# Five of eight heads' retrieval queries and half of an embedding gate moved between the expert rows of block 0; eight gather slots outside the activations

## What is computed

```
q = (h @ w_q).reshape(B, S, 8, 2, 128)
s1, s2 = q[..., 0, :] @ sub_k1, q[..., 1, :] @ sub_k2      # scores against 128 keys each
v1, i1 = top_k(s1, 16); v2, i2 = top_k(s2, 16)
top_s, pos = top_k(v1[..., :, None] + v2[..., None, :], 16)  # 16 experts a head
wts = softmax(top_s)
act = gelu(einsum('thkd,td->thk', u_tab[idx], h))
out = einsum('thk,thkd->td', act * wts, v_tab[idx])
ple = sigmoid(h @ ple_gate) * (p @ ple_proj)
h = layer_norm(alpha * h + out + ple)
```

## Time and profile before

| | us |
|---|---|
| median of 3 runs (2114.31 to 2115.43) | 2114.32 |
| the profiled execution's own time | 2115.31 |
| its span, first to last instruction | 2113.5 |
| PE busy | 1796.5 (85%) |
| DVE busy | 1407.9 (67%) |
| ACT busy | 992.0 (47%) |
| POOL busy | 765.5 (36%) |

### The profile page before, as it was taken

How to read it: one execution, slowest core, us unless ns; L and a number is a source line. 1 busy time by engine, 2 the same in 40 slices (tenths; PEclk the granted TensorE clock), 3 DMA queues, 4 the chain that set the end, 5 groups by cost and what they waited for, 6 DMA issues and landing times.

```text
span 2113.5 us, 29001 instructions
## 1 busy us (share of the span) xinstructions
PE 1796.5 (85%) x6952; PEld 1054.8 (50%) x6952; DVE 1407.9 (67%) x3374; ACT 992.0 (47%) x2295; POOL 765.5 (36%) x614
## 2 busy tenths in 40 slices
PE   8999999978787787787799899998888877878876
PEld 7988778822232222222289887787323322323222
DVE  5864555677777677776558645566777776777764
ACT  5644354454554544444346443444445454444443
POOL 0020000146555556655400300001565655665553
PEclk9999999999999999999999999999999999999999
DMA  7422445789999999999844233456899999999997
GB/s 259 145 101 92 138 140 190 276 354 428 427 427 428 427 427 428 427 428 427 371 137 144 90 110 130 151 188 249 352 427 428 428 427 427 427 427 428 428 427 319
DMA packets 106126, 659.43 MB, mean 312 GB/s; under 512 B 11824, under 2 KB 11968, under 8 KB 39616
## 3 DMA queue, kind: packets, MB, share of 16 engines
q0 software_dynamic: 75232, 545.52, 61.5%
q1 hardware_dynamic: 30816, 112.91, 15.8%
HBM read 657.32 MB, written 1.06 MB: 312 GB/s over the span
## 4 chain that ended last, share of the span: by engine, by line
DMA 22%; PE 21%; issue 9%; DVE 5%; ACT 5%; POOL 2%; DVEq 0%; POOLq 0%; ACTq 0%
DMA arena<-experts_dram,stage 17%; PE acc L593 7%; DMA hidden<-experts_dram,stage 4%; PE psum L544 4%; PE psum L546 3%; PE psum L545 3%; DVE arena L1273 1%; ACT arena L924 1%; POOL arena L510 1%; DVE arena L1244 1%; ACT gw L921 1%; ACT w_hi L858 1%; DMA raw<-weights_dram 1%; POOL stage L507 1%; DVE arena L1117 1%
## 5 line engine op out<-in xcount | busy, mean ns | idle before, releaser
L593 PE MATMUL acc<-arena 128*128 128x512 f32 x1536 | 764.0, 628 | 233.8 <-ACT arena L924 224.8
L510 POOL DMA_INDIRECT arena<-experts_dram,stage x384 | 526.1, 1370 | 342.5 <-PE acc L593 223.0
L1244 DVE CUSTOM_DVE_ANT_0 arena<-arena,h 128x1024 f32<-128x1024 f32 x384 | 471.1, 1227 | 248.0 <-DMA arena<-experts_dram,stage 162.3
L593 PEld LDWEIGHTS acc<-arena 128*128 128x128 f32 x1536 | 273.8, 194 | 715.2 <-issue 714.8
L918 ACT ACTIVATE gel<-dots 128x1 f32<-128x1 f32 x512 | 103.3, 202 | 520.3 <-DVE dots L1244 519.5
L1152 DVE TENSOR_TENSOR raw_r<-raw,w_hi 128x1024 fp32r<-128x1024 f32 x200 | 237.1, 1222 | 148.9 <-ACT w_hi L858 147.9
L858 ACT ACTIVATE w_hi<-raw 128x1024 fp32r<-128x1024 f32 x200 | 203.7, 1055 | 158.6 <-DMA raw<-weights_dram 128.2
L593 PE MATMUL acc<-hidden,arena 128*128 128x512 f32 x512 | 245.0, 612 | 29.8 <-ACT arena L924 27.4
L924 ACT ACTIVATE arena<-cst,gw 128x128 f32<-128x128 f32 x512 | 205.8, 402 | 87.7 <-ACT gw L921 37.0
L510 POOL DMA_INDIRECT hidden<-experts_dram,stage x128 | 163.7, 1279 | 137.3 <-PE acc L593 95.5
L1244 DVE CUSTOM_DVE_ANT_0 hidden<-hidden,h 128x1024 f32<-128x1024 f32 x128 | 157.3, 1229 | 74.5 <-issue 45.8
(11 more groups left out here) (256 smaller groups left out, 2052.3 us busy)
## 6 DMA issues: line engine op xcount, KB each, us to landing
raw<-weights_dram SPq DMA_DIRECT2D x208, 512.0 KB, 3.4
arena<-experts_dram,stage POOLq DMA_INDIRECT x384
lnr<-lnrows_dram POOLq DMA_DIRECT2D x4, 1024.0 KB, 5.3
arena<-cum_dram POOLq DMA_DIRECT2D x2, 1024.0 KB, 9.3
hidden<-experts_dram,stage POOLq DMA_INDIRECT x128
cst<-consts_dram SPq DMA_DIRECT2D x1, 1640.0 KB, 15.3
par<-params_dram POOLq DMA_DIRECT2D x2, 616.0 KB, 11.1
h<-x_dram SPq DMA_DIRECT2D x2, 512.0 KB, 5.4
```

The source lines that it names most:

```text
L510: nc.gpsimd.indirect_dma_start(slots[i % RING][:, :], None, experts[:, :], bass.IndirectOffsetOnAxis(stage[:, i:i + 1], 0)).then_inc(slot_ ...
L593: last = mm(acc[:, c * 512:(c + 1) * 512], diag[:, i % 4, :], slots[i % RING][:, D + c * 512:D + (c + 1) * 512], start=False, stop=ends)
L1244: nc.vector.tensor_tensor_reduce(slots[s][:, 0:D], slots[s][:, 0:D], h[:, b, :], 1.0, 0.0, ALU.mult, ALU.add, dots[:, i:i + 1]).then_inc(d ...
```

## The change

- `steps()`: head by head. Three heads' queries and scores come first, each head in two half steps (`wqh`, `wq`) and two score steps (`sc`, b, head), with `select` 0 and 1 between them; then the first half of the gate, in quarters (`pgw`), and then the 128 rows of block 0 as steps of their own. Beside head r of them stand head r + 3's half steps after rows 3 and 6 and its scores after row 9 (r from 0 to 4), and beside head 5 the gate's other half after rows 3, 6, 9 and 12. Block 1 stays in the loop.
- `group_list()`: the pieces come in that order; keys in four half pieces of 256 KB. High halves stand at rows 0 and 2, low halves at rows 1 and 3 of a head.
- The rows of block 0 are straight code on every engine; POOL reads `idxu` directly, without the copy to `stage`.
- Slots 6 and 7 are no longer in `hidden`, for both blocks: one lies in the arena, one over 2048 columns of the constants, which only the dense stage reads. POOL reloads them (1 MB) after the last row of layer 0, and the users in layer 1 wait for it (`dense_consts`). The queries keep four tiles, used in turn, outside the slots.
- POOL's waits for the last scores and the last gate product go; what is left are the head's indices and `row_used`. DVE waits for a head's scores where it selects.

```diff
-    s += [("wq", 0, 0), ("pp", 1, 1), ("wq", 0, 1), ("wq", 1, 0), ("wq", 1, 1)] + [("sc", b, g) for g in range(2) for b in range(2)]
-    s += [("select", 0), ("texp", 0), ("wq", 2, 0), ("wq", 2, 1), ("wq", 3, 0), ("wq", 3, 1)]
-    s += [("sc", b, g) for g in range(2, 4) for b in range(2)]
-    s += [("pg", 0, 0), ("pg", 0, 1), ("select", 1), ("texp", 1), ("pg", 1, 0), ("pg", 1, 1)]
-    s += [("experts", 0), ("ln2", 0), ("experts", 1), ("ln2", 1)]
+    s += [("wqh", 0, 0), ("wq", 0, 0), ("pp", 1, 1), ("sc", 0, 0), ("sc", 1, 0), ("select", 0)]
+    s += [("wqh", 0, 1), ("wq", 0, 1), ("sc", 0, 1), ("sc", 1, 1), ("texp", 0), ("select", 1)]
+    s += [("wqh", 1, 0), ("wq", 1, 0), ("sc", 0, 2), ("sc", 1, 2), ("texp", 1)]
+    s += [("pgw", 0, j) for j in range(4)] + [("pg", 0, 0), ("pg", 0, 1)]
+    beside = {(hd - 3, 3): [("wqh", hd // 2, hd % 2)] for hd in range(3, EH)}
+    beside |= {(hd - 3, 6): [("wq", hd // 2, hd % 2)] for hd in range(3, EH)}
+    beside |= {(hd - 3, 9): [("sc", 0, hd), ("sc", 1, hd)] for hd in range(3, EH)}
+    beside |= {(5, 3 + 3 * j): [("pgw", 1, j)] for j in range(4)}
+    beside[5, 12] += [("pg", 1, 0), ("pg", 1, 1)]
+    for r in range(EH):
+        for i in range(TOPK):
+            s += [("row", r, i)] + beside.get((r, i), [])
+    s += [("ln2", 0), ("experts", 1), ("ln2", 1)]
...
+    put_splits(at, ("wq", 1, 0), (("wq", 0, 1), ("wq", 0, 1)))
+    put_splits(at, ("pg", 0, 0), (("texp", 0), ("texp", 0), ("texp", 1), ("texp", 1)))
...
-        slots += [hidden[:, 2 * D * i:2 * D * (i + 1)] for i in range(2)]
-        qpT = at(4096, 4096).rearrange("p (k t) -> p k t", k=16)
+        slots += [at(15648, 2 * D), cst[:, C_LEV:C_LEV + 2 * D]]
+        qpT = at(20320, 1024).rearrange("p (k t) -> p k t", k=4)
...
+                    if kind == "row":
+                        _, r, i = step
+                        n = r * TOPK + i
+                        if i == 0:
+                            pool.wait_ge(idx_ready, L * NB * EH + r + 1)
+                        pool.wait_ge(row_used, L * NB * RANKS + n + 1)
+                        nc.gpsimd.indirect_dma_start(
+                            slots[n % RING][:, :], None, experts[:, :],
+                            bass.IndirectOffsetOnAxis(idxu[:, n:n + 1], 0)).then_inc(slot_in[n % RING], 16)
...
+                        pool.wait_ge(acc_filled, NB * (L + 1))
+                        pool.dma_start(cst[:, C_LEV:C_LEV + 2 * D], consts[:, C_LEV:C_LEV + 2 * D]).then_inc(consts_back, 16)
...
+                        act.wait_ge(dot_ready, n0 + n + 1)
+                        AC(gel[:, i:i + 1], dots[:, i:i + 1], ACT.Gelu).then_inc(dot_used, 1)
+                        act.wait_ge(dot_used, n0 + n + 1 + TOPK)
+                        link(AC(gw[:, i:i + 1], gel[:, i:i + 1], ACT.Copy, scale=wts[:, n:n + 1]))
+                        act.wait_ge(row_used, n0 + n + RING - 3)
+                        AC(diag[:, i % 4, :], ident, ACT.Copy, scale=gw[:, i:i + 1]).then_inc(diag_ready, 1)
```

More of the change, by code:

```diff
@@ L173, with dense_splits @@
 COUNTED = [(i, j) for i, j in PIECES if GROUPS[i][2][j] is None]
-def splits():
-    order = [i for i, g in enumerate(GROUPS) if g[1]]
+def dense_splits(lo):
+    order = [i for i, g in enumerate(GROUPS) if g[1] and g[0][0][0] not in ("wq", "pg")]
     at = {}
@@ new lines, in feature_major, with gate_piece @@
+            def feature_major(L, g, ps, p):
+                feature_half(L, g, ps, 2 * p, 0)
+                return feature_half(L, g, ps, 2 * p + 1, 1)
+            def gate_piece(L, c, j, blocks):
+                w = split(L, GROUP_OF["pg", c, 0], j)
+                for ps, b in blocks:
+                    for i in range(2):
+                        k = 2 * j + i
+                        ends[b] = mm3(ps, [hT[:, i2, k, b * P:(b + 1) * P] for i2 in range(2)], [x[:, i * 512:(i + 1) * 512] for x in w], k == 0, k == KT - 1)
+                read(L, GROUP_OF["pg", c, 0], j, ends[1])
@@ L1224, in _ @@
                         continue
+                    if kind == "row":
+                        _, r, i = step
+                        n = r * TOPK + i
+                        if i == 0:
+                            choose = select_head(L, r + AHEAD)
+                        dve.wait_ge(dot_used, L * NB * RANKS + n + 1)
+                        dve.wait_ge(*landed(L, n))
+                        slot = slots[n % RING]
+                        nc.vector.tensor_tensor_reduce(slot[:, 0:D], slot[:, 0:D], h[:, 0, :], 1.0, 0.0, ALU.mult, ALU.add, dots[:, i:i + 1]).then_inc(dot_ready, 1)
+                        if i == 0:
+                            if r + AHEAD < EH:
+                                dve.wait_ge(*drained(L, ("sc", 0, r + AHEAD)))
+                            elif r + AHEAD == EH:
+                                for hd in range(EH):
+                                    dve.wait_ge(*drained(L, ("sc", 1, hd)))
+                        next(choose, None)
+                        if i == TOPK - 1:
+                            for _ in choose:
+                                pass
+                        continue
                     if kind == "experts":
@@ L1227, in _ @@
                         n0 = (L * NB + b) * RANKS
-                        g0 = (L * NB + b) * EH
-                        for q in range(1, 8):
-                            dve.wait_ge(*drained(L, ("sc", q % 2, q // 2)))
                         def head(r, beside, looped):
```

214 lines of the change are left out of this document (132 added, 82 removed).

## The result

| | before | after |
|---|---|---|
| median of the runs, us | 2114.32 (4 runs, 2113.12 to 2115.43) | 2087.85 (4 runs, 2086.63 to 2089.71) |
| profiled execution: own time, span | 2115.31, 2113.5 | 2088.15, 2086.3 |
| PE / DVE / ACT / POOL busy | 1796.5 / 1407.9 / 992.0 / 765.5 | 1783.1 / 1404.2 / 942.9 / 724.9 |
| moved, mean over the span | 659.43 MB, 312 GB/s | 660.72 MB, 317 GB/s |

The ratio is 0.9874, with a 95% interval from 0.9858 to 0.9889: faster by 26.5 us, where I had forecast 30.5. The last pair of experiments adds that the same program gained only 17.6 us in a later measurement.

What follows compares the result with a forecast made beforehand. Gathers filling the DMA engines, started late, were taken as the bound. Two restarts 41.2 us earlier, less 43.9 for pieces and 4 a layer for gaps, gave 30.5 off 2114.32: 2084 us, own range 2075 to 2096, whole range 2064 to 2108.

Steps and rivals of the forecast that it cites:

- restart: Ninth gather of a layer, first needing a slot freed by PE: 41.2 us earlier in each layer (394.4, not 435.6).
- pieces: Weight loads still to be issued after the restart, 20 in layer 0, 13 in layer 1, at 1.33 us: cost 43.9 us.
- plateau: Stretch of some 600 us per layer, from the restart on, with the 16 DMA engines full at 427 to 428 GB/s.
- gaps: DMA time lost to dense work on PE, 3 us just after the restart and 1 in head 5: 4 us a layer.
- slack of 3 us either way: Uncertainty given to the chain up to the restart, chiefly which half VectorE gets to first: some 3 us.
- Only the restart in the sum: The start's gain was counted by the restart's move alone, 41.2 us a layer; earlier first gathers were not priced.
- The hand-offs: At each drain of queries or scores beside the rows, PE waits 2.2 us for ACT's drain and three small operations.
- Costed at nothing: VectorE's low halves, ACT's high halves, the 1 MB constants reload, the fourth key piece and the unrolled code: 0 us.
- Fully covered: Rival, chance 0.2: no gap after the restart and pieces at 428 GB/s, gain 42 us, 2072 us.
- Thin gain: Rival, chance 0.17: pieces at 1.55 us, 10 us of gaps a layer, or a chain 3 us later; 2103 us.
- The row chain: Rival, chance 0.07: drains empty the ring, dense time is exposed and row work becomes the bound; slower, about 2140 us.

Runs made afterwards that it cites:

- The last pair of experiments: The changed kernel unaltered, and one with the gate's second half spread over heads 5 and 6, run together on another chip: 2096.57 and 2095.94 us.
- experiment 2: The changed kernel with the first gather held until the first half of the gate is in its banks: 2105.79 us.
- experiment 8: The changed kernel with the whole gate beside the rows and VectorE's two operations on a drained gate bank behind the next row's dot: 2070.50 us.
- experiment 1: The kernel before with only its two last slots moved, the constants reloaded, and no wait for the gate ahead of the seventh gather: 2117.54 us.

## Why the prediction was right, and where it was off

The mechanism was right: an earlier restart, paid for with pieces in the plateau. That the sum was only 3.3 us off, by the spans, is in part luck: the restarts gave 3.1 us more than I had and the pieces cost 3.3 less, and the gaps cost 9.7 more. Layer 0's last gather came 11.7 us earlier, where I had 11, by the same cancelling; layer 1's came a further 15.5, where I had 20.

- **The restart, 41.2 us.** Right: 44.0 and 41.5. The steps stood as told: first gather 360.2 (361.3), second selection's halves 374.9 (376.0), row 0's dot 383.9 (386.5). The last quarter of the gate ended 0.8 us sooner than I had it, and the first sigmoid and its two operations ran beside that quarter and the second sigmoid, where I had them one after the other; from dot to restart it took 7.7 us (7.9). But "slack of 3 us either way" was too small: on the last chip the restart comes 4.4 us later in layer 0 (1.6 of it ahead of the first gather) and 3.6 in layer 1, and 17.6 us of gain are left in place of 26.5. At 2096.57 us the same program lies just above the forecast's own range of 2075 to 2096, though within the whole range, which ends at 2108.
- **Only the restart in the sum.** Right for this change, wrong as a measure: experiment 2 moves the restart by 4.2 and the layer by 9.0 us. It held since the first eight gathers had landed when the ninth went out, before and after.
- **The pieces, 43.9 us.** The count of 20 and 13 was exact by the bytes; the price of 1.33 was too high. The way I read it was at fault, and not the window: in the changed plateau the piece queue's share gives 1.30 us again (10.49 MB for 4.1% of 634.7 us), while leaving the bytes out frees 1.21 there. A queue's share of the engines' time is not what the span pays for it; why they differ is not shown. At 426 GB/s it is 1.23, 40.6 us in all. The estimate by the ceiling of the Trainium skill, "DMA: Bandwidth & Descriptors", "Where 436 GB/s comes from" (1.20 us) was nearer than my row; no plateau reaches the ceiling of 435.2 itself, they run at 425 to 428.
- **The gaps, 4 us a layer.** The term that failed: 7.7 and 10.0 us. Behind the restart it was about right: the hole there is 5.8 us in layer 0, but 3.6 stood there before as well, which I had overlooked, so 2.2 and 2.4 us are new, where I had 3. Head 5 loses nothing in layer 0 and 4.6 us in layer 1, where I had 1 each. The rest, the slots' 1.4 us a layer, the one more gather of layer 0 and 1.7 and 1.6 us without a row, I did not have at all. I had priced PE's time there (43.3 us a head), but not the order on ACT and DVE that puts the gate's drains ahead of a row's dot, nor the halved clock behind a wait of 4.3 us.
- **The hand-offs.** I had 2.2 us of PE's waiting at each drain; its waits for diagonals are 1.2 us each, 29 of them from 390 to 630 us, 34.7 us in all. Nothing came of them but at the two holes, since the DMA queue covers them, as said.
- **Costed at nothing.** High halves waited for pieces once, 0.6 us, though these landed after 11.0 us, not 8.7. The reload of the constants shows in no wait of another engine. The new slots, which the sum leaves out, were not nothing.
- **The rivals.** Fully covered (2072) failed on the two holes; it is what the version of experiment 8 comes to by another way. Thin gain (2103): the 2096.6 us on the last chip lie toward it, by one of its three conditions, a chain some 3 us later, though for a reason that I did not see, the late word. The row chain never became the bound.

## What to carry to other kernels

Where a transfer plateau bounds a kernel, count bytes in it and the time for which its queue is empty; the time of one restart stands for that only when nothing is queued across it. Dense work beside such a plateau is covered while the queue is deep, and is exposed just behind a restart and wherever a drain stands ahead of the row in the order of two engines at once: put the row first. The same program differed by 8.7 us between two measurements, and the kernel before did not, so a gain should be measured more than once and on more than one chip. That it is the idle TensorE in the chain which makes it so is a guess.

## What the runs showed of the hardware

- The same program took 2087.85 us in the first measurement and 2096.57 in a later one, with the kernel before at 2114.3 and 2114.2 beside it. Of the difference, 6.7 us stand between the first gather and the restart of the two layers, behind one product that ACT hears of 2.6 and 3.4 us after its record's end. Over all the kernels that had it the delay was 1.3 to 3.6 us, and it was there at full clock too.
- Two gather slots at other addresses took the plateau from 427 to 428 GB/s down to 426, 1.4 us a layer, with the same bytes (experiment 1). Which of the two does it is open.
- Behind an idle stretch of 4.3 us the granted clock stood at half for 5 us, and two rows took 3.2 us each in place of 1.8, so that the wait cost 2.8 us more than itself, and the gathers' slots came free later.
